# Gate matrix of a PEER layer stored as groups of 16 expert rows with the tokens outside, instead of expert rows with the tokens inside

## The chip, the cores and the metric

The kernel runs on one core of one Trainium2 chip. The metric is device time in microseconds (us) of one execution. The kernel before took 1841.26 us, the median of three runs (1835.47 to 1842.40).

## The reference, cut to what matters

One decoder layer for 576 tokens (512 of a prompt, 64 of samples), model width 1024. After attention, convolution and their output projection comes PEER: each token picks, in each of 8 heads, 16 of 16384 single-neuron experts. Expert e = i * 128 + j has a row u[e] and a row v[e].

```python
best_s, pos = lax.top_k(cand_s, PEER_TOPK)
idx = jnp.take_along_axis(cand_i, pos, axis=-1)
gate = jax.nn.softmax(best_s, axis=-1)
...
hu = jnp.einsum('chkd,cd->chk', jnp.take(u, ib, axis=0), xb)
act = jax.nn.gelu(hu, approximate=False) * gb
return jnp.einsum('chk,chkd->cd', act, jnp.take(v, ib, axis=0))
```

## The kernel before, in words

The tokens are split. For the last 192 tokens (tiles 3 and 4) the rows of u and v are gathered from memory one pick at a time: 384 rows of 128 tokens x 1024, each an indirect DMA issued by POOL into an eight-slot ring and one VectorE instruction (L1349 for u, L1353 for v). For the first 384 tokens PEER is computed densely, over all experts, in 128 blocks n of 128 experts:

- the U part: `dense_u(n)` multiplies a block of u with the tokens (24 matmuls of 384 columns, L711), ScalarE applies gelu into `gest` (`step`, L942), and SyncE stores it to `gelu_matrix` in memory (`store_gelu`, L402);
- the gate matrix: for each token an expert-by-expert matrix of gates, 128 partitions (i) x 128 rows (j);
- the V part: the gelu block and the gate block of n are loaded and multiplied on VectorE into `mt` (L1420), and 18 matmuls of 512 columns (L783) add the product with a block of v into PSUM.

Weights and activations of both dense parts are split in a high and a low half: ScalarE rounds (`high`, L916; `ah`, L1026), VectorE subtracts (`low`, L1234; `al`, L1428). `raw`, the block as it comes from memory, has three buffers; `hi`, `lo`, `mt`, `ah` and `al` have two.

The gate matrix is built in 64 batches of six tokens (`NBAT`, `BATCH`). For each batch VectorE writes two sets of one-hot rows, `gA` and `gB` (L1397, three buffers, `ABUF`), ScalarE scales `gA` by the gates (L997, six instructions), TensorE multiplies the two for each token (L761), giving 128 x 128 per token in PSUM, and ScalarE copies the six results into `Gs` (L1013). Four batches fill one block of 24 tokens (`TBLK`), of which there are 16 (`NBLK`), and SyncE then stores it to `gate_matrix` (L469). Between the batches each engine's program has a share of other work written out by hand: 54 blocks of the U part (`u_at`), 126 gathered rows of u and 26 of v (`batch_rows`). Below, "the gate stage" is the stretch of these 64 batches, about 893 to 1252 us of the profiled execution, and "the V stage" what follows the last five blocks of the U part, about 1283 to 1837 us.

In the V stage the gates are used in groups g of 16 expert rows j (`JG`): `Gl` holds two groups, each with 16 blocks of 24 tokens. Step n uses row n % 16 of group n // 16. The sixteen block loads of group g + 1 are issued one a step during group g, each right behind the multiplication of that step (`sp.wait_ge(s_mu, n + 1)`, then `load_gelu(n + EG)`, then `load_gates(n // JG + 1, n % JG)`), so the last one of a group is issued after the multiplication of its 16th step and is needed by the next one. VectorE's program for a step is: `mt` (L1420), one gathered row of v, `low`, `al`, and in about three steps of ten (`v_rows`) one more gathered row; 166 rows in 128 steps. ScalarE's is `high` for step n, which waits until TensorE is through with step n - 2, and then `ah`. TensorE waits for `low` and `al` of the step.

Of the kernel before, what the change touches and what calls it, by code (L numbers as in the profile page):

```python
# [5 lines left out]
ALU = mybir.AluOpType  # L6
# [8 lines left out]
P = 128  # L15
# [18 lines left out]
NKEY = 128  # L34
# [11 lines left out]
TBLK = 24  # L46
NBLK = DT // TBLK
BATCH = 6
ABUF = 3
NBAT = DT // BATCH  # L50
JG = 16
NG = NKEY // JG
# [117 lines left out]
def hymba_peer(nc, xT_d, wblk_d, cols_d, maskp_d, masks_d, ident_d, ckT_d, cv_d, state_d, keysT_d, u_d, v_d, uT_d,  # L170
# [7 lines left out]
    with ExitStack() as ctx:  # L178
        def sb(name, shape, dt=F32):
            return ctx.enter_context(nc.sbuf_tensor(name, shape, dt))[:]  # L180
# [4 lines left out]
        ps = [ctx.enter_context(nc.psum_tensor(f"ps{i}", [P, 1024], F32)) for i in range(4)]  # L185
# [11 lines left out]
        with ExitStack() as gates:  # L197
            def gb(name, shape, dt=F32):
                return gates.enter_context(nc.sbuf_tensor(name, shape, dt))[:]

            kT3 = gb("kT3", [P, 3, DT])
            A = gb("gA", [P, ABUF, BATCH, NKEY])
            B = gb("gB", [P, ABUF, BATCH, NKEY])
            Gs = gb("Gs", [P, 2, NKEY, TBLK])

        Gl = sb("Gl", [P, 2, NBLK, JG, TBLK])
        cols = sb("cols_sb", [P, NCOL])
        ident = sb("ident_sb", [P, P])
        epst = sb("epst", [P, 1])
# [157 lines left out]
        def _(sp):  # L367
# [47 lines left out]
                sp.dma_start(gel[:, n % EG, :], ge_d[k][:, (n % 2) * DT:(n % 2 + 1) * DT]).then_inc(e_in[n % EG], 16)  # L415

            def load_gates(g, b):
                sp.dma_start(Gl[:, g % 2, b].rearrange("p j t -> p (j t)"),
                             gm_d[b, :, g * JG:(g + 1) * JG, :].rearrange("p j t -> p (j t)")).then_inc(s_gl[g % 2], 16)

            for c in range(DC):
                sp.dma_start(hT[:, c, :], xT_d[:, c, :]).then_inc(x_in[c], 16)
# [40 lines left out]
            for b in range(NBAT):  # L463
                for n in range(u_at(b), u_at(b + 1)):
                    after_u(n)
                if b % (TBLK // BATCH) == TBLK // BATCH - 1:
                    i = b // (TBLK // BATCH)
                    sp.wait_ge(s_gev, b + 1)
                    sp.dma_start(gm_d[i].rearrange("p j t -> p (j t)"),  # L469
                                 Gs[:, i % 2].rearrange("p j t -> p (j t)")).then_inc(s_gst, 16)  # L470

            for n in range(U_TAIL, NKEY):
                after_u(n)
# [30 lines left out]
        def _(pe):  # L504
# [49 lines left out]
            n = nblk[0]  # L554
# [199 lines left out]
            for b in range(NBAT):  # L754
                pe.wait_ge(s_ab, 2 * b + 2)
                pe.wait_ge(s_ag, b + 1)
                if b >= ABUF:
                    pe.wait_ge(s_gev, b - ABUF + 1)
                for t in range(BATCH):
                    c = (t // 3) * 512 + (t % 3) * NKEY  # L760
                    mm = nc.tensor.matmul(ps[b % ABUF][:, c:c + NKEY], A[:, b % ABUF, t, :], B[:, b % ABUF, t, :],  # L761
                                          start=True, stop=True)
                mm.then_inc(s_gmm, 1)
                for n in range(u_at(b), u_at(b + 1)):
                    dense_u(n)
# [23 lines left out]
        def _(act):  # L789
# [212 lines left out]
            for b in range(NBAT):  # L1002
                i = b // (TBLK // BATCH)
                o = b % (TBLK // BATCH) * BATCH
                if b + 1 < NBAT:
                    apply_gates(b + 1)
                act.wait_ge(s_gmm, b + 1)
                if o == 0 and i >= 2:
                    act.wait_ge(s_gst, 16 * (i - 1))
                dst = Gs[:, i % 2, :, o:o + BATCH].rearrange("p j (a t) -> p a t j", a=2)  # L1010
                src = ps[b % ABUF][:, :].rearrange("p (a c) -> p a c", a=2)[:, :, 0:3 * NKEY].rearrange(
                    "p a (t j) -> p a t j", t=3)
                nc.scalar.activation(dst, src, ACT.Copy).then_inc(s_gev, 1)  # L1013
                if b in GELU_AFTER:
                    gelu_rows(GELU_AFTER[b])
                for n in range(u_at(b), u_at(b + 1)):
                    step(n)
# [43 lines left out]
        def _(dve):  # L1061
# [351 lines left out]
            for n in range(NKEY):  # L1413

                g = n // JG
                dve.wait_ge(e_in[n % EG], 16 * (n // EG + 1))
                dve.wait_ge(s_gl[g % 2], 16 * NBLK * (g // 2 + 1))
                if n >= 2:
                    dve.wait_ge(s_al, n - 1)
                nc.vector.tensor_tensor(mt[:, n % 2, :].rearrange("p (a b) -> p a b", a=NBLK),  # L1420
                                        gel[:, n % EG, :].rearrange("p (a b) -> p a b", a=NBLK),
                                        Gl[:, g % 2, :, n % JG, :], ALU.mult).then_inc(s_mu, 1)
                rows = list(range(v_rows(n), v_rows(n + 1)))
                for r in rows[:1]:
                    row(r)
                low(NKEY + n)
                dve.wait_ge(s_ah, n + 1)
                nc.vector.tensor_tensor(al[:, n % 2, :], mt[:, n % 2, :], ah[:, n % 2, :].bitcast(F32),  # L1428
                                        ALU.subtract).then_inc(s_al, 1)
                for r in rows[1:]:  # L1430
                    row(r)
                if UROW + NPICK in range(v_rows(n), v_rows(n + 1)):
                    dve.wait_ge(g_used, UROW + NPICK)
                    dve.sem_inc(s_y, 1)
# [98 lines left out]
```

## Time and profile before

| | |
|---|---|
| median of three runs | 1841.26 us (1835.47 to 1842.40) |
| profiled execution | 1849.16 us, span in the trace 1847.3 us |
| granted TensorE clock, mean | 0.953 |
| busy: PE, DVE, ACT, POOL | 1669.8, 1432.0, 770.1, 550.0 us |
| DMA over the span | 477.45 MB, mean 258 GB/s |

PE is TensorE (PEld its weight loads), DVE VectorE, ACT ScalarE, POOL GpSimd, SP SyncE, which here only issues DMAs. All times are of one profiled execution; the busy share of an engine over the whole span is an average over stages with different limits, so the stages are read apart. "Idle before" is time in which the engine did nothing before an instruction, and the name behind the arrow what ended it, as far as the semaphores show.

### The profile page before, as it was taken

What the parts mean: (1) busy time and instruction counts of PE and PEld (TensorE: products, weight loads), DVE (VectorE), ACT (ScalarE), POOL (GpSimd) and SP (SyncE); (2) the same over time, 40 slices, a digit from 0 to 9 for tenths busy, and PEclk for the clock granted to TensorE, in tenths of its full rate; (3) what the DMA queues carried; (4) which work ended last, traced back from release to release, by engine and by line L of the source; (5) the groups of instructions that cost most, each with busy time, mean ns of one, the idle gap of its engine ahead of it and who ended that gap; (6) DMA issues with size and microseconds to landing.
All of it is one profiled execution on the core that took longest, in us unless ns stands there. A gap on an engine that the chain in (4) does not pass through costs nothing.

```text
span 1847.3 us, 23140 instructions
## 1 busy us (share of the span) xinstructions
PE 1669.8 (90%) x8361; PEld 1447.9 (78%) x8361; DVE 1432.0 (78%) x2657; ACT 770.1 (42%) x1274; POOL 550.0 (30%) x395
## 2 busy tenths in 40 slices
PE   7887678989699998999889898998999999999997
PEld 5766446769697877999889898998877877877876
DVE  3466854338778999787899999994888888988976
ACT  3222112212242222444789888883333333333332
POOL 0000000000011333111477676661344443443430
PEclk9998887999899999999999999999999999999999
DMA  6110500125275877777699999999999999999985
GB/s 192 46 46 1 66 1 13 50 68 194 89 247 184 277 281 228 248 235 234 216 415 407 406 413 402 381 403 389 363 371 371 375 362 381 387 358 365 379 306 184
DMA packets 164360, 477.45 MB, mean 258 GB/s; under 512 B 28063, under 2 KB 61535, under 8 KB 162071
## 3 DMA queue, kind: packets, MB, share of 16 engines
q1 hardware_dynamic: 108951, 274.63, 42.7%
q0 software_dynamic: 55296, 201.35, 28.7%
q8 instruction: 67, 1.10, 0.2%
q14 instruction: 46, 0.38, 0.1%
HBM read 420.93 MB, written 54.42 MB: 257 GB/s over the span
## 4 chain that ended last, share of the span: by engine, by line
PE 55%; DVE 33%; issue 5%; ACT 3%; DMA 2%; SPq 0%; DVEq 0%; ACTq 0%
PE ps L783 24%; PE ps L711 14%; PE ps L524 9%; DVE ring L1349 8%; DVE lo L1234 4%; DVE acc L1353 2%; DVE gA L1397 2%; DVE gB L1397 2%; DVE cacc L1457 2%; DVE tsi L1246 2%; PE ps L536 2%; DVE tsi L1249 2%; DVE sm L1247 2%; DVE tsv L1248 1%; DMA gelu_matrix<-gest 1%
## 5 line engine op out<-in xcount | busy, mean ns | idle before, releaser
L1057 POOL DMA_INDIRECT ring<-in_u,idx x192 | 281.6, 1467 | 889.1 <-DVE ijg L1329 528.4
L1234 DVE TENSOR_TENSOR lo<-raw,hi 128x1024 fp32r<-128x1024 f32 x256 | 312.9, 1222 | 138.3 <-ACT hi L916 132.2
L916 ACT ACTIVATE hi<-raw 128x1024 fp32r<-128x1024 f32 x256 | 270.4, 1056 | 330.7 <-PE ps L783 323.9
L711 PE MATMUL ps<-xh,hi 128*128 128x384 f32 x1024 | 356.1, 348 | 28.2 <-DVE lo L1234 20.2
L1057 POOL DMA_INDIRECT ring<-in_v,idx x192 | 266.9, 1390 | 369.4 <-DVE acc L1353 351.2
L711 PE MATMUL ps<-xl,hi 128*128 128x384 f32 x1024 | 348.0, 340 | 0.0
L711 PE MATMUL ps<-xh,lo 128*128 128x384 f32 x1024 | 347.5, 339 | 0.0
L783 PE MATMUL ps<-hi,ah 128*128 128x512 f32 x768 | 241.6, 396 | 23.1 <-DVE al L1428 23.0
L1353 DVE SCALAR_TENSOR_TENSOR acc<-ring,hu,acc 128x1024 f32<-128x1024 f32 x192 | 245.6, 1279 | 1.6
L783 PE MATMUL ps<-lo,ah 128*128 128x512 f32 x768 | 240.0, 394 | 0.0
L783 PE MATMUL ps<-hi,al 128*128 128x512 f32 x768 | 239.6, 394 | 0.0
L1349 DVE CUSTOM_DVE_ANT_0 ring<-ring,xtok 128x1024 f32<-128x1024 f32 x192 | 226.2, 1216 | 0.3 <-DVE hu L1349 0.3
L711 PEld LDWEIGHTS ps<-xh,hi 128*128 128x128 f32 x1024 | 197.7, 193 | 31.0 <-DVE lo L1234 22.9
L711 PEld LDWEIGHTS ps<-xl,hi 128*128 128x128 f32 x1024 | 197.2, 193 | 0.0
L711 PEld LDWEIGHTS ps<-xh,lo 128*128 128x128 f32 x1024 | 196.6, 192 | 0.0
L783 PEld LDWEIGHTS ps<-hi,ah 128*128 128x128 f32 x768 | 146.2, 191 | 56.6 <-DVE lo L1234 20.9
L783 PEld LDWEIGHTS ps<-lo,ah 128*128 128x128 f32 x768 | 146.6, 191 | 31.1
L783 PEld LDWEIGHTS ps<-hi,al 128*128 128x128 f32 x768 | 146.3, 190 | 31.0
L942 ACT ACTIVATE gest<-ps 128x384 f32<-128x384 f32 x128 | 63.4, 495 | 251.8 <-PE ps L711 210.7
L681 PE MATMUL ps<-xn,wring 128*128 128x192 f32 (+1 forms) x512 | 133.6, 416 | 5.6 <-DVE xn L1224 5.6
L1013 ACT ACTIVATE Gs<-ps 128x768 f32<-128x768 f32 x64 | 132.3, 2067 | 0.5 <-PE ps L761 0.5
L761 PE MATMUL ps<-gB,gA 128*128 128x128 f32 x768 | 103.3, 288 | 32.0 <-issue 18.4
(176 smaller groups left out, 1971.8 us busy)
## 6 DMA issues: line engine op xcount, KB each, us to landing
raw<-in_uT SPq DMA_DIRECT2D x128, 512.0 KB
raw<-in_v SPq DMA_DIRECT2D x128, 512.0 KB
wring<-in_wblk SPq DMA_DIRECT2D x48, 512.0 KB
gelu_matrix<-gest SPq DMA_DIRECT2D x64, 384.0 KB
gate_matrix<-Gs SPq DMA_DIRECT2D x16, 1536.0 KB
Gl<-gate_matrix SPq DMA_DIRECT2D x128, 192.0 KB
gel<-gelu_matrix SPq DMA_DIRECT2D x128, 192.0 KB
wring<-in_wblk SPq DMA_DIRECT2D x16, 256.0 KB
```

The costliest lines, as they stand in the source:

```text
L524: mm = nc.tensor.matmul(out[:, a * 512:a * 512 + HALF], w, rhs[:, k, a * HALF:(a + 1) * HALF], start=(k == 0), stop=(k == kc - 1))
L681: mm = nc.tensor.matmul(out[:, 0:w], wring[:, n % RING, k * P:(k + 1) * P], xn[:, k, t0:t0 + w], start=(k == 0), stop=(k == DC - 1))
L711: mm = nc.tensor.matmul(out, a[:, n % 2, w], b[:, c, :], start=(c == 0 and k == 0), stop=(c == DC - 1 and k == 2))
L761: mm = nc.tensor.matmul(ps[b % ABUF][:, c:c + NKEY], A[:, b % ABUF, t, :], B[:, b % ABUF, t, :], start=True, stop=True)
L783: mm = nc.tensor.matmul(ps[t][:, h * 512:(h + 1) * 512], a[:, n % 2, w], b[:, n % 2, h * 512:(h + 1) * 512], start=False, stop=(n == NKEY ...
L916: nc.scalar.activation(hi[:, s % 2, :], raw[:, s % RAWS, :], ACT.Copy).then_inc(s_hi, 1)
L1013: nc.scalar.activation(dst, src, ACT.Copy).then_inc(s_gev, 1)
L1057: pool.indirect_dma_start(ring[:, r % SLOTS, :], None, table, bass.IndirectOffsetOnAxis(idx[:, t, c:c + 1], 0)).then_inc(g_in[r % SLOTS], 16)
L1234: nc.vector.tensor_tensor(lo[:, s % 2, :], raw[:, s % RAWS, :], hi[:, s % 2, :].bitcast(F32), ALU.subtract).then_inc(s_lo, 1)
L1349: nc.vector.tensor_tensor_reduce(got, got, xtok[:, t, :], 1.0, 0.0, ALU.mult, ALU.add, hu[:, t, c:c + 1]).then_inc(g_used, 1)
L1353: nc.vector.scalar_tensor_tensor(out=acc[:, t, :], in0=got, scalar=hu[:, t, c:c + 1], in1=acc[:, t, :], op0=ALU.mult, op1=ALU.add).then_in ...
L1397: nc.vector.tensor_tensor(dst[:, b % ABUF], iota.unsqueeze(1).broadcast_to([P, BATCH, NKEY]), kT3[:, half, tok:tok + BATCH].unsqueeze(2).b ...
```

## The change

The layout of the gate matrix is changed in all four places where it is touched: in `Gs`, in memory, in `Gl`, and in the operand of the multiplication.

- In `Gs` a token's 128 gates of a partition lay 24 elements (96 bytes) apart, with the tokens next to each other. Now they lie in eight groups of 16 adjacent elements (64 bytes); within a group the tokens follow one another, so the groups of a block are 1536 bytes each.
- The store writes the same 12288 contiguous bytes of each partition, and a load still reads and writes 1536 contiguous bytes of each partition. The number and size of the DMAs and their places in the queue are unchanged.
- In PSUM the six results of a batch lay as three and three, each three at the start of a bank of 512; now they lie one behind the other, four in the first bank and two in the second.
- The multiplication L1420 read 16 runs of 24 adjacent gates for its 384 tokens. Now it reads 384 single gates, each 16 elements (64 bytes) from the one before. Its other input and its output are as before.

No instruction is added, removed or moved on any engine: the programs of PE, DVE, ACT, POOL and SP have the same instructions in the same order with the same waits, and only the access patterns named above differ.

```diff
-            Gs = gb("Gs", [P, 2, NKEY, TBLK])
+            Gs = gb("Gs", [P, 2, NG, TBLK, JG])
-        Gl = sb("Gl", [P, 2, NBLK, JG, TBLK])
+        Gl = sb("Gl", [P, 2, NBLK, TBLK, JG])
...
             def load_gates(g, b):
-                sp.dma_start(Gl[:, g % 2, b].rearrange("p j t -> p (j t)"),
-                             gm_d[b, :, g * JG:(g + 1) * JG, :].rearrange("p j t -> p (j t)")).then_inc(s_gl[g % 2], 16)
+                sp.dma_start(Gl[:, g % 2, b].rearrange("p t j -> p (t j)"),
+                             gm_d[b].rearrange("p j t -> p (j t)")[:, g * JG * TBLK:(g + 1) * JG * TBLK]).then_inc(
+                                 s_gl[g % 2], 16)
...
                     sp.dma_start(gm_d[i].rearrange("p j t -> p (j t)"),
-                                 Gs[:, i % 2].rearrange("p j t -> p (j t)")).then_inc(s_gst, 16)
+                                 Gs[:, i % 2].rearrange("p g t j -> p (g t j)")).then_inc(s_gst, 16)
...
                 for t in range(BATCH):
-                    c = (t // 3) * 512 + (t % 3) * NKEY
+                    c = t * NKEY
...
-                dst = Gs[:, i % 2, :, o:o + BATCH].rearrange("p j (a t) -> p a t j", a=2)
-                src = ps[b % ABUF][:, :].rearrange("p (a c) -> p a c", a=2)[:, :, 0:3 * NKEY].rearrange(
-                    "p a (t j) -> p a t j", t=3)
+                dst = Gs[:, i % 2, :, o:o + BATCH, :].rearrange("p g t j -> p t g j")
+                src = ps[b % ABUF][:, 0:BATCH * NKEY].rearrange("p (t g j) -> p t g j", t=BATCH, g=NG)
                 nc.scalar.activation(dst, src, ACT.Copy).then_inc(s_gev, 1)
...
                 nc.vector.tensor_tensor(mt[:, n % 2, :].rearrange("p (a b) -> p a b", a=NBLK),
                                         gel[:, n % EG, :].rearrange("p (a b) -> p a b", a=NBLK),
-                                        Gl[:, g % 2, :, n % JG, :], ALU.mult).then_inc(s_mu, 1)
+                                        Gl[:, g % 2, :, :, n % JG], ALU.mult).then_inc(s_mu, 1)
```

## Rows read from the trace of the kernel before

**Rows 1.** Stretches: length, busy us (instructions) of each engine, granted clock, DMA share, GB/s

```profile
900.00:1000.00 100.00, 93.20 (x595) 92.69 (x595) 100.00 (x141) 88.30 (x158) 73.13 (x44) 0.96 0.97 382
...
1280.00:1840.00 560.00, 534.75 (x2304) 439.15 (x2304) 473.50 (x553) 191.79 (x261) 213.65 (x157) 0.98 0.94 352
```

**Rows 2.** Groups of instructions, shapes kept apart: count | busy us, mean ns | idle before

```profile
L1013 ACT ACTIVATE Gs<-ps 128x768 f32<-128x768 f32 x64 | 132.3, 2067 | 0.5 <-PE ps L761 0.5
L942 ACT ACTIVATE gest<-ps 128x384 f32<-128x384 f32 x128 | 63.4, 495 | 251.8 <-PE ps L711 210.7 <-DMA gelu_matrix<-gest 22.0 <-issue 19.1
L849 ACT ACTIVATE PTb<-ps 128x1024 f32<-128x1024 f32 x6 | 6.1, 1024 | 49.7 <-PE ps L601 49.7
...
L761 PE MATMUL ps<-gB,gA 128*128 128x128 f32 x768 | 103.3, 288 | 32.0 <-issue 18.4 <-DVE gA L1397 9.4 <-ACT gA L997 4.2
```

**Rows 3.** Waits between 893 and 1252 us: us in total, times, longest

```profile
DVE lo L1234 <- ACT hi L916: 6.0, 4, 2.1
...
ACT gest L942 <- DMA gelu_matrix<-gest: 12.8, 6, 5.5
```

**Rows 4.** Timeline before one of these waits, SP, ACT and DVE: start, length, idle before

```profile
1004.95 0.33 SPq L469 DMA_DIRECT2D gate_matrix<-Gs  x1
...
1005.79 1.33 SPq L402 DMA_DIRECT2D gelu_matrix<-gest  x1
...
1019.48 0.49 ACT L942 ACTIVATE gest<-ps 128x384 f32<-128x384 f32 x1 [5.49 <-DMA gelu_matrix<-gest]
...
1020.94 1.23 DVE L1234 TENSOR_TENSOR lo<-raw,hi 128x1024 fp32r<-128x1024 f32 x1 [2.11 <-ACT hi L916]
```

**Rows 5.** Timeline from the last batch to the V stage, ACT and SP

```profile
1249.14 2.08 ACT L1013 ACTIVATE Gs<-ps 128x768 f32<-128x768 f32 x1
...
1251.25 0.33 SPq L469 DMA_DIRECT2D gate_matrix<-Gs  x1
...
1270.63 0.42 SPq L402 DMA_DIRECT2D gelu_matrix<-gest  x1
...
1279.74 0.49 ACT L942 ACTIVATE gest<-ps 128x384 f32<-128x384 f32 x1 [7.80 <-DMA gelu_matrix<-gest]
```

**Rows 6.** Groups of VectorE's instructions, shapes kept apart, columns as in rows 2

```profile
L1420 DVE TENSOR_TENSOR mt<-gel,Gl 128x384 f32<-128x384 f32 x128 | 70.6, 552 | 29.3 <-issue 26.6 <-DMA gel<-gelu_matrix 2.7
L1234 DVE TENSOR_TENSOR lo<-raw,hi 128x1024 fp32r<-128x1024 f32 x256 | 312.9, 1222 | 138.3 <-ACT hi L916 132.2 <-issue 2.9
```

**Rows 7.** Timeline of VectorE over steps 15 to 18 of a group

```profile
1479.76 0.55 DVE L1420 TENSOR_TENSOR mt<-gel,Gl 128x384 f32<-128x384 f32 x1
...
1489.14 0.56 DVE L1420 TENSOR_TENSOR mt<-gel,Gl 128x384 f32<-128x384 f32 x1 [4.02 <-issue]
...
1492.42 0.55 DVE L1420 TENSOR_TENSOR mt<-gel,Gl 128x384 f32<-128x384 f32 x1
1492.89 1.28 DVE L1353 SCALAR_TENSOR_TENSOR acc<-ring,hu,acc 128x1024 f32<-128x1024 f32 x1
1494.08 1.22 DVE L1234 TENSOR_TENSOR lo<-raw,hi 128x1024 fp32r<-128x1024 f32 x1
...
1495.69 0.55 DVE L1420 TENSOR_TENSOR mt<-gel,Gl 128x384 f32<-128x384 f32 x1
```

**Rows 8.** Timeline of ScalarE in steady steps of the V stage

```profile
1501.11 1.06 ACT L916 ACTIVATE hi<-raw 128x1024 fp32r<-128x1024 f32 x1 [2.61 <-PE ps L783]
...
1529.67 1.07 ACT L916 ACTIVATE hi<-raw 128x1024 fp32r<-128x1024 f32 x1 [2.61 <-PE ps L783]
```

**Rows 9.** Chain of waits: TensorE's restarts after the first and the seventh group

```profile
1353.52 4.34 PE ps L783 x18
...
1768.51 68.17 PE ps L783 x288
```

**Rows 10.** Waits between 1300 and 1837 us, VectorE: us in total, times, longest

```profile
DVE lo L1234 <- ACT hi L916: 46.6, 74, 3.3
DVE mt L1420 <- issue: 26.6, 7, 4.4
```

## The prediction

> **What bounds the kernel now.** I read the stretches first [rows 1]. In the gate stage VectorE is the full engine, 100.00 us of the 100 between 900 and 1000 us, ScalarE follows at 88.30, and TensorE, though busy by its records for 93.20, waits for the other two between batches. In the V stage TensorE is busy for 534.75 of 560 us, VectorE for 473.50, ScalarE for only 191.79. The change touches ScalarE in the first stage and VectorE in the second, so both are worked out apart.
>
> In the steady part of the V stage ScalarE starts `hi` eight times in 28.56 us, always released by TensorE, so a step takes 28.56 / 7 = 4.08 us [rows 8]. VectorE's own program for such a step is shorter: from one `mt` to the next without a wait 1495.69 - 1492.42 = 3.27 us with one gathered row, whose place in it is 1.19 us [rows 7]. With 166 rows in 128 steps there are 0.297 more rows a step, so 3.27 + 0.297 x 1.2 = 3.63 us. VectorE has 0.45 us a step to spare, and it shows as 46.6 us of waits of `lo` for `hi` [rows 10]. TensorE bounds the steady steps.
>
> Once a group there is another limit. The last load of the next group's gates is issued behind the 16th `mt`, and the next `mt` starts 1489.14 - 1479.76 = 9.38 us after it, with VectorE idle for the last 4.02 us [rows 7], 26.6 us in seven boundaries [rows 10]. TensorE's restarts after the first and the seventh boundary give the length of a group: (1768.51 - 1353.52) / 6 = 69.2 us [rows 9]. Were VectorE never to wait for `hi`, a group would take 15 x 3.63 + 9.38 = 63.8 us.
>
> **The copy L1013.** It takes 2067 ns for 768 elements, while contiguous activations out of PSUM take 495 ns for 384 and 1024 ns for 1024 [rows 2]. The slope is 529 / 640 = 0.83 ns an element with about 178 ns fixed, so the copy pays (2067 - 178) / 768 = 2.46 ns an element where 0.83 would be the price of adjacent ones. What is peculiar in it is the 96-byte step of its output. In the new layout its output comes in runs of 16 adjacent elements, and I price it at 178 + 768 x 0.83 = about 815 ns: 1.25 us less each, 64 x 1.25 = 80 us less of ScalarE's work. The bounds are 0 and 1.25 us saved; I take 1.25: the row of 1024 elements, which crosses the end of a PSUM bank, shows no price for that, and that jumps between runs of 16 cost nothing is my choice.
>
> Almost none of the 80 us lies on the path. VectorE is full there, with work that the change leaves alone. All it can gain is its waits for `hi`, 6.0 us in four pieces [rows 3]. One of them shows how they come about: SyncE stands at the store of a gate block until the fourth copy is done, behind it stand a load of `raw` and a store of gelu, the latter issued at 1005.79; ScalarE waits for it until 1019.48, and VectorE at 1020.94 [rows 4]. A copy that ends 1.25 us earlier moves the queue up by that. Still, 13.7 us from issue to release is mostly a loaded memory path, with the DMA share at 0.97 in the stretch before [rows 1], and that load stays. Behind the stage the last copy (1249.14), the last gate store (1251.25), the gate loads behind it, the gelu store (1270.63) and the gelu step (1279.74) are one chain into the V stage, which moves up by 1.25 us with the copy [rows 5]. So the gate stage gives between 0 and 6.0 + 1.25 = 7.3 us; I take 4. TensorE's write of six results to other columns of PSUM and the DMAs, the same in number and bytes, I cost at nothing: nothing about them changes that could be slower, and TensorE has its waits for VectorE as cover in that stage; without that cover L761 slower by a tenth would cost a tenth of its 103.3 us [rows 2].
>
> **The multiplication L1420.** It takes 552 ns for 384 elements, and `lo` takes 1222 ns for 1024 [rows 6], so VectorE runs at 670 / 640 = 1.05 ns an element. Its second input is now read at a 64-byte step. No instruction of VectorE in the trace reads singly at such a step. The bounds are no cost at all (the rate it has in all its other forms) and the increment of the copy, (2.46 - 0.83) x 384 = 0.63 us. Since the row nearest to it, and the only one of single fp32 elements far apart, shows 2.46 ns an element, I take that rate as one of the memory, whatever the engine: (2.46 - 1.05) x 384 = 0.54 us more, `mt` at about 1.09 us. Call this extra x.
>
> What x does to a group: VectorE's own length becomes 63.8 + 16x, and the length set by TensorE 69.2 + 2x, because around a boundary the 16th `mt` (before the last load) and the next one (after it) are both on the path. They cross at x = 0.38. Below that only 2x a boundary is paid, above it VectorE sets the group. With x = 0.54 it is 63.8 + 8.6 = 72.4 us, 3.2 more than 69.2. Seven groups end in a boundary: 22.4 us. The eighth has none: 15 steps x (3.63 + 0.54 - 4.08) = 1.4 us. Sum of the V stage: +24 us. ScalarE's `ah` waits for `mt` but is needed only by `al`, behind a row and `low`, so its chain costs nothing more; the row gathers of POOL and the loads behind `s_mu` on SP come later by x each step, with four buffers of `gel` and eight of the ring as cover.
>
> **Weighing the skill.** By the trace a step of 96 bytes costs 2.46 ns an element on ScalarE's output [rows 2]. The Trainium skill, "Vector Engine (DVE) Microarchitecture Reference", section 5.2, gives for VectorE 2.50 to 2.51 ns a column where both sources, or the output alone, step by 24 words, but only 1.73 where one source hops by 4 KiB each element and the rest is contiguous. With 1.73 the extra would be an estimated (1.73 - 1.05) x 384 = 0.26 us, under the crossing; with 2.50 an estimated 0.56. The trace of before shows neither for VectorE, and the step of 64 bytes stands in neither line.
>
> **Sum.** 24 - 4 = +20 us: 1849.16 + 20 = 1869 for the profiled execution. That execution was 7.9 us above the median of the runs shown, so the forecast against the median is 1841.26 + 20 = 1861.
>
> **Rivals.**
> 1. *VectorE reads at a middling price, x up to 0.38, and its slack covers it.* For it: 0.45 us of idle time a step [rows 7, 8]. Against it: the rate of the copy. With x = 0.27, half of what I take, it costs 7 x 0.54 = 3.8 us, and some 2 more where two-row steps follow closely, less 4 from the gate stage: 1843, a range of 1836 to 1849.
> 2. *The read costs nothing and the kernel gets faster.* The place is ScalarE's copy and the chain of waits behind it, the price of the V stage is zero, and it decides as long as 14x stays under the gate stage's gain, so for x below about 0.3 if that gain is 4. For it: the copy is slow on its output, and nothing in the trace shows a slow input; an output that must put single words into a wider line may be a case of its own. Against it: the small share of ScalarE on the path. Time: 1841 - 4 = 1837, at best 1834 with all 7.3 us. The Trainium skill, "VectorE: DVE Perf Modes", in its part on the one-element mode, says that this mode makes no assumptions and that fp32 and weird strides work in it. By that rule, this rival is the outcome; no row of the trace contradicts it.
> 3. *The step of 64 bytes costs more than the one of 96.* With x = 0.63 a group is 73.9 us and the V stage 7 x 4.7 + 15 x 0.18 = +36; with nothing gained in the gate stage the time is 1877. If the price were a whole copy-like fixed wait per element more (x = 0.8), a group would be 76.6 and the time about 1895. Against it: no row is that slow.
> 4. *The copy doesn't get faster,* since its output still has two levels of jumps. Then the gate stage gives 0, and with x = 0.54 the time is 1865. The new output's runs speak against it.
>
> **Chances.** Forecast, with rival 4 as a variant of it: 0.56 (0.06 of it rival 4). Rival 1: 0.20. Rival 2: 0.12. Rival 3: 0.12. The range 1837 to 1877 leaves out the better half of rival 2, some of rival 1 and the upper half of rival 3, together near 0.2. The likeliest case has its own range, 1851 to 1872: its V stage lies between +15 (x = 0.47) and +31 (x = 0.6), its gate stage between 0 and -5. Half a per cent, 9.2 us, is about what a measurement of this kernel can tell from no change. Faster than 1832 needs rival 2 with more than the chain seen can give: 0.05. Slower than 1850.5: the forecast but for its low end, rival 3, a rest of rival 1: 0.54 + 0.12 + 0.02 = 0.68. Between them 0.27.
>
> **What would show it.** In the profile after: L1013 at about 0.82 us and ScalarE at about 690 us in all; L1420 at 1.09 us instead of 552 ns; the waits of `lo` for `hi` in the V stage down from 46.6 us to a few; TensorE waiting inside the groups for `al` or `lo`, and its restarts 72.4 us apart; the 26.6 us at the boundaries unchanged; in the gate stage VectorE waiting less than 6.0 us for `hi`. An `mt` under 0.9 us proves the forecast wrong, and so does a group of 70 us with an `mt` over a microsecond, since then VectorE's slack was not what I count.

## The result, and the profile after

The changed kernel takes 1853.62 us, the median of 11 runs (1842.35 to 1858.31), against 1842.46 us of the kernel before in the same call (11 runs). The ratio on record is 1.0044, 95% interval 1.0023 to 1.0065: 8 us slower (4 to 12), where the two medians alone lie 11 us apart; the text goes by the ratios. Forecast were 20 us and a time of 1861 us. The profiled execution took 1849.48 us, 4 us under the median of its kind, and the profiled one of before 7 us over its own, so the two traces, 0.3 us apart, don't show the loss in their totals. They show what happened to each step.

The stretches after, columns as in [rows 1]:

```profile
900.00:1000.00 100.00, 94.35 (x600) 93.83 (x600) 100.00 (x141) 65.56 (x155) 73.10 (x44) 0.96 0.97 382
1280.00:1840.00 560.00, 532.42 (x2301) 435.73 (x2299) 501.16 (x549) 188.39 (x255) 299.46 (x157) 0.98 0.94 348
```

ScalarE fell from 88.30 to 65.56 us in the stretch of the gate stage with VectorE still at 100.00, and VectorE rose from 473.50 to 501.16 us in the V stage. POOL rose there from 213.65 to 299.46 us, which I had not expected. The groups, columns as in [rows 2, 6]:

```profile
L1013 ACT ACTIVATE Gs<-ps 128x768 f32<-128x768 f32 x64 | 50.9, 796 | 2.4 <-PE ps L762 2.4
L1420 DVE TENSOR_TENSOR mt<-gel,Gl 128x384 f32<-128x384 f32 x128 | 105.5, 824 | 31.8 <-issue 28.7 <-DMA gel<-gelu_matrix 3.1
L1057 POOL DMA_INDIRECT ring<-in_v,idx x192 | 354.3, 1845 | 286.8 <-DVE acc L1353 272.8 <-issue 9.8 <-DVE hu L1349 4.2
```

The copy takes 796 ns instead of 2067, against 815 forecast. The multiplication takes 824 ns instead of 552, so x is 0.27 us, half of the 0.54 that I took. The waits between 893 and 1252 us:

```profile
DVE lo L1234 <- ACT hi L917: 2.6, 1, 2.6
```

They were 6.0 us in four pieces [rows 3]. All four are gone: the one left is the wait that stood just behind the end of this stretch before. The trace of before, then that of after:

```profile
1254.12 1.22 DVE L1234 TENSOR_TENSOR lo<-raw,hi 128x1024 fp32r<-128x1024 f32 x1 [2.65 <-ACT hi L916]
```

```profile
1248.15 1.22 DVE L1234 TENSOR_TENSOR lo<-raw,hi 128x1024 fp32r<-128x1024 f32 x1 [2.63 <-ACT hi L917]
```

The V stage's first `mt` starts at 1270.30 us in this trace, at 1275.95 before: 5.7 us earlier, where I took 4. All `mt` of the V stage, before and then after (count, shortest/mean/longest in ns, first and last start in us):

```profile
L1420 DVE TENSOR_TENSOR mt<-gel,Gl x128: 548/551/559, 1275.9 to 1827.2; 128x384 f32<-128x384 f32 x128
```

```profile
L1420 DVE TENSOR_TENSOR mt<-gel,Gl x128: 801/824/854, 1270.3 to 1827.7; 128x384 f32<-128x384 f32 x128
```

From the first to the last it is 551.3 us before and 557.4 after. So the gain of the gate stage is there, and a V stage 6.1 us longer takes it back. VectorE's steps in the V stage after, as in [rows 7]:

```profile
1475.05 0.82 DVE L1420 TENSOR_TENSOR mt<-gel,Gl 128x384 f32<-128x384 f32 x1
...
1484.39 0.80 DVE L1420 TENSOR_TENSOR mt<-gel,Gl 128x384 f32<-128x384 f32 x1 [3.98 <-issue]
...
1487.91 0.81 DVE L1420 TENSOR_TENSOR mt<-gel,Gl 128x384 f32<-128x384 f32 x1
...
1491.44 0.83 DVE L1420 TENSOR_TENSOR mt<-gel,Gl 128x384 f32<-128x384 f32 x1
```

A step with one gathered row is 1491.44 - 1487.91 = 3.53 us, 0.26 more than before, and still under TensorE's 4.08.

### The profile page after: what moved, and what is told of

Read it like the earlier page. It is cut to its first block, busy times and chain, and to the rows that moved or that the text cites. A ratio compares the mean times of both kernels' runs of the same rounds, so it can differ in the third digit from the quotient of the medians.

```text
span 1847.7 us, 23140 instructions
## 1 busy us (share of the span) xinstructions
PE 1669.4 (90%) x8361; PEld 1445.4 (78%) x8361; DVE 1463.5 (79%) x2657; ACT 692.6 (37%) x1274; POOL 638.9 (35%) x395
## 4 chain that ended last, share of the span: by engine, by line
PE 51%; DVE 36%; issue 5%; DMA 4%; ACT 3%; SPq 0%; DVEq 0%; POOL 0%; ACTq 0%
PE ps L784 21%; PE ps L712 13%; DVE ring L1349 9%; PE ps L525 9%; DVE lo L1234 4%; DVE acc L1353 2%; DVE gA L1397 2%; DVE gB L1397 2%; DVE cacc L1457 2%; PE ps L537 2%; DVE tsi L1246 2%; DVE tsi L1249 2%; DVE sm L1247 2%; DVE tsv L1248 1%; DMA gelu_matrix<-gest 1%
## 5 line engine op out<-in xcount | busy, mean ns | idle before, releaser
L1057 POOL DMA_INDIRECT ring<-in_v,idx x192 | 354.3, 1845 | 286.8 <-DVE acc L1353 272.8
L1420 DVE TENSOR_TENSOR mt<-gel,Gl 128x384 f32<-128x384 f32 x128 | 105.5, 824 | 31.8 <-issue 28.7
```

The source lines that it names most:

```text
L1057: pool.indirect_dma_start(ring[:, r % SLOTS, :], None, table, bass.IndirectOffsetOnAxis(idx[:, t, c:c + 1], 0)).then_inc(g_in[r % SLOTS], 16)
```

## The experiments

All ratios are to the kernel before in the same call, with 95% intervals; 0.001 is 1.8 us.

**The two halves of the change apart.** `mul_only` is the kernel before with another view in the multiplication, `copy_only` the changed one (views shortened):

```diff
-  Gl[:, g % 2, :, n % JG, :]                                   # before
+  Gl[:, g % 2] as "p (b t j) -> p b t j" [:, :, :, n % JG]     # mul_only
-  Gl[:, g % 2, :, :, n % JG]                                   # after
+  Gl[:, g % 2] as "p (b j t) -> p b j t" [:, :, n % JG, :]     # copy_only
```

> The kernel before, but the multiplication L1420 reads its gates singly at a 64-byte step, so it multiplies by gates of other tokens and experts; the copy and the layout stay as before. Theory A (the changed kernel is slower only through the multiplication, whose extra 0.27 us is mostly covered by VectorE's slack): mt at 0.82 us, the V stage longer by 14 x 0.27 = 3.8 us at the boundaries and by what close two-row steps cost, together +4 to +14 us, nothing gained in the gate stage, so +4 to +14 us against before, more than the changed kernel itself by the gate stage's 4 to 6 us. Rival B (the multiplication is covered, and what makes the changed kernel slower is a shift of the transfers against each other that begins in the gate stage): within 3 us of before.

Measured: 1.0039 (1.0017 to 1.0061), +7 us, with the multiplication at 825 ns. Theory A's range holds it; rival B's (3 us) ends just where the interval begins.

> The changed kernel, but the multiplication L1420 reads runs of 24 adjacent gates from the new layout, so it multiplies by gates of other tokens and experts; copy, store and loads are as changed. Theory A: the gate stage ends 4 to 6 us earlier as in the changed kernel, L1420 back at 0.55 us, V stage as before: -4 to -6 us against before. Rival B (the earlier gate stage is given back in the V stage by transfers): 0 to +8 us against before with a V stage longer than before's although L1420 takes 0.55 us.

Measured: 0.9975 (0.9952 to 0.9998), -4.6 us (-9 to 0), as theory A had it.

**Another way to a fast copy.** The kernel before with `dst = Gs[:, i % 2, :, o:o + BATCH]`, `src = ps[...][:, 0:768].rearrange("p (t j) -> p j t", t=BATCH)` and `c = t * NKEY`:

> The kernel before with its layout of the gate matrix and its multiplication; the copy L1013 goes through its elements in another order, experts outside and the six tokens inside: it writes runs of six adjacent elements (24 bytes) and reads PSUM at a step of 512 bytes, the six results lying one behind the other. If only the output's single elements make the copy slow, it takes about 0.8 us and the kernel has the gain of the gate stage without the slower multiplication: -4 to -6 us. If steps in PSUM cost as steps in the output do, the copy takes 1.5 to 2.1 us and the time is that of before within 3 us.

Measured: 0.9972 (0.9944 to 1.0000), -5 us; the copy takes 830 ns. The time alone would not exclude the other theory, the duration does: steps of 512 bytes in PSUM cost it next to nothing (830 against 796 ns); its single elements in the output did.

**What a step costs.** One profile, eight forms of each instruction, every form on a line of its own:

> The changed kernel with eight forms of the multiplication L1420, one for each n % 8 (adjacent gates; single gates 8, 16, 32, 64, 96 and 128 bytes apart; pairs of adjacent gates 128 bytes apart), and eight forms of the copy L1013, one for each block % 8 (adjacent; single elements 16, 32, 64, 96 and 128 bytes apart; pairs 192 bytes apart; runs of six from PSUM at 512 bytes); the gates used are others than the reference's. For the theory of my prediction that one rate of the memory holds for all engines, the multiplication at 96 bytes should take about 1.1 us although it takes 0.82 at 64. If VectorE's input simply costs less than ScalarE's output, 64, 96 and 128 bytes all take about 0.82 us. Adjacent forms and pairs: 0.55 us and 0.8 us.

The groups of that profile, multiplication first. L1462 is adjacent, L1464 to L1474 are 8, 16, 32, 64, 96 and 128 bytes apart, L1476 pairs 128 bytes apart. L1022 is adjacent, L1024 to L1036 are 16, 32, 64, 96 and 128 bytes apart, L1038 pairs 192 bytes apart. The multiplications at 96 and 128 bytes read 192 elements twice, the others 384 different ones.

```profile
L1472 DVE TENSOR_TENSOR mt<-gel,Gl 128x384 f32<-128x384 f32 x16 | 17.7, 1109 | 0.0
L1033 ACT ACTIVATE Gs<-ps 128x768 f32<-128x768 f32 x8 | 16.5, 2064 | 0.0
L1468 DVE TENSOR_TENSOR mt<-gel,Gl 128x384 f32<-128x384 f32 x16 | 14.3, 892 | 0.0
L1474 DVE TENSOR_TENSOR mt<-gel,Gl 128x384 f32<-128x384 f32 x16 | 14.2, 885 | 0.0
L1466 DVE TENSOR_TENSOR mt<-gel,Gl 128x384 f32<-128x384 f32 x16 | 13.5, 844 | 0.0
L1027 ACT ACTIVATE Gs<-ps 128x768 f32<-128x768 f32 x8 | 13.4, 1674 | 0.0
L1470 DVE TENSOR_TENSOR mt<-gel,Gl 128x384 f32<-128x384 f32 x16 | 13.2, 824 | 0.0
L1036 ACT ACTIVATE Gs<-ps 128x768 f32<-128x768 f32 x8 | 12.7, 1589 | 0.0
L1024 ACT ACTIVATE Gs<-ps 128x768 f32<-128x768 f32 x8 | 12.5, 1560 | 0.0
L1030 ACT ACTIVATE Gs<-ps 128x768 f32<-128x768 f32 x8 | 12.3, 1543 | 0.0
L1462 DVE TENSOR_TENSOR mt<-gel,Gl 128x384 f32<-128x384 f32 x16 | 8.9, 555 | 35.8 <-issue 32.0 <-DMA gel<-gelu_matrix 3.8
L1476 DVE TENSOR_TENSOR mt<-gel,Gl 128x384 f32<-128x384 f32 x16 | 8.9, 554 | 0.0
L1464 DVE TENSOR_TENSOR mt<-gel,Gl 128x384 f32<-128x384 f32 x16 | 8.8, 552 | 0.0
...
L1038 ACT ACTIVATE Gs<-ps 128x768 f32<-128x768 f32 x8 | 6.9, 863 | 0.0
...
L1022 ACT ACTIVATE Gs<-ps 128x768 f32<-128x768 f32 x8 | 6.4, 800 | 0.8 <-PE ps L762 0.8
```

Both theories of the expectation were half right. The 96-byte step does have one rate on both engines: 1.05 + (1109 - 552) / 384 = 2.50 ns an element on VectorE, (2064 - 178) / 768 = 2.46 on ScalarE, and my figure of 1.09 us would have been right for it. But 96 bytes is a special step. At 16, 32, 64 and 128 bytes the two take 1.76 to 1.94 and 1.78 to 1.95 ns. Single elements 8 bytes apart and pairs 128 bytes apart cost VectorE nothing, and pairs 192 bytes apart cost ScalarE 63 ns of 800. The figures of the Trainium skill that the prediction names ("Vector Engine (DVE) Microarchitecture Reference", section 5.2) agree with this: its 2.50 to 2.51 for a step of 24 words is stated for both sources or the output, and one source alone shows 2.50 here; its 1.73 for one source hopping by 4 KiB is close to the 1.76 of the 64-byte step.

**The same with x = 0.56.** The multiplication reads `Gl[...][0:4608]` at every 24th element, 192 elements twice:

> The kernel before, with the multiplication L1420 reading single gates 96 bytes apart (the wrong gates, 192 of them twice); by the sweep it takes 1.11 us, so x = 0.56 us. My sum (VectorE's own length of a group 63.8 + 16x against TensorE's 69.2 + 2x) gives groups of 72.8 us and 7 x 3.6 + 15 x 0.11 = +27 us against before. If what VectorE's extra costs is simply proportional to it (7 us for 0.27 us), +15 us. If transfers set the V stage rather than either engine, +7 to +10 us as with x = 0.27.

Measured: 1.0063 (1.0040 to 1.0086), +12 us, multiplication 1106 ns. My sum (+27) is out; the transfers' +7 to +10 and the proportional +15 both lie in the interval.

**Both halves, old layout.** Fast copy as above, slow multiplication as in `mul_only`:

> The kernel before with the copy's experts outside and tokens inside (0.83 us) and with the multiplication reading singly at a 64-byte step (0.82 us, the wrong gates): both of the change's effects without its layout. If the two add up, +7.2 - 5.2 = +2 us against before. If there is something in having both (the earlier start of the V stage is lost where VectorE has less slack), or the changed kernel's +8 us is the true sum, +6 to +10 us. If it comes out at +2 while the changed kernel is at +8, the layout itself costs something.

Measured: 1.0050 (1.0031 to 1.0069), +9 us, like the changed kernel. So no cost of the layout in memory shows, within some 5 us. The halves alone sum to +2.6 us, with some 6 us of uncertainty on that sum, so that they don't add up is suggested by this and not shown.

> Copy with experts outside (0.83 us) and multiplication reading single gates 96 bytes apart (1.11 us, wrong gates). If gate stage and V stage add up: +11.6 with the slow copy, less 5.2 = +6 us. If the gain of the fast copy is lost whenever VectorE has little slack (as +9 instead of +2 at 0.82 us suggests), +12 to +18 us.

The edit is that of the 96-byte multiplication in the kernel with the fast copy. Measured: 1.0055 (1.0031 to 1.0079), +10 us, with the slow copy it was +12. The gain of 5 us that the fast copy has with the fast multiplication is not seen in the time with the slow one; but +6 is just within the interval too, so this is open.

**Groups of 2 expert rows.** `Gs [P, 2, NKEY // 2, TBLK, 2]`, `Gl [P, 2, NBLK, JG // 2, TBLK, 2]`:

> The changed kernel with groups of 2 expert rows instead of 16 in Gs, memory and Gl (tokens outside a pair, a load still 1536 adjacent bytes): the copy writes pairs of adjacent elements, the multiplication reads single gates 8 bytes apart. By the sweep the copy takes 0.86 us and the multiplication 0.55 us. If only the two durations matter, it is where the copy alone was, 0.9975 of before (-5 us), though tokens lie outside as in the changed kernel. If the layout in memory has a price of its own, +3 us or more against before.

Measured: 0.9984 (0.9959 to 1.0009), multiplication 552 ns, copy 869 ns. That is -3 us (-8 to +2): the interval holds the first expectation (-5) and not the second (+3 or more), so tokens outside cost nothing that shows.

**The boundary off the path.** SyncE's loads of the next group's gates come closer together:

```diff
-   if n // JG + 1 < NG:
-       load_gates(n // JG + 1, n % JG)
+   if n // JG + 1 < NG and n % JG < NBLK // 2:       # early
+       load_gates(n // JG + 1, 2 * (n % JG))
+       load_gates(n // JG + 1, 2 * (n % JG) + 1)
+   # spread: n % JG < 12; blocks 2k and 2k + 1 for k < 4, then block k + 4
```

> The changed kernel, but SyncE issues two gate loads of the next group in each of the first eight steps of a group instead of one in each of the sixteen, so the last has eight steps to land. If the boundary wait is the last load alone, the 28.7 us of waits of mt at the boundaries go and with them 20 to 28 us of the kernel (-12 to -20 us against before), and the 2x at each boundary is off the path. If the memory path is the limit there, the loads that come closer together delay raw and gel by as much and the time stays within 5 us of the changed kernel (0 to +12 against before).

> The kernel with the copy's experts outside and tokens inside (fast copy, multiplication at 0.55 us), and gate loads two a step as in the other run of this call. If VectorE's slack covers the extra 0.27 us of the multiplication once the boundaries are off the path, this is within 4 us of the changed kernel with early gate loads, less the clash of two-row steps, -15 to -30 us against before. If the extra is uncovered within the groups, this is 7 to 12 us faster than the changed kernel with early gate loads.

Measured: 0.9945 (0.9922 to 0.9968) and 0.9912 (0.9885 to 0.9938), -10 and -16 us. The waits of `mt` at the boundaries are gone, but less than their 28 us was won, and the second kernel is only 6 us (within some 6) ahead of the first, between the two expectations. ScalarE waits for `raw` for 97 and 102 us in the V stage, against 15 in the changed kernel.

> Fast copy with experts outside, multiplication at 0.55 us, and the sixteen gate loads of the next group issued in the first twelve steps (two in each of the first four, then one). With two in each of the first eight steps, ScalarE waited 102 us for raw and the boundary was free. If the crowding of the loads costs, this is 3 to 8 us faster than that, 0.987 to 0.989 of before; if the memory path is full over the whole group, it is the same, 0.991.

> The changed kernel (multiplication 0.82 us) with the gate loads of the next group spread over the first twelve steps. Against the same spread with the multiplication at 0.55 us (0.9834 of before). If VectorE's slack of 0.45 us a step covers the extra 0.27 us once the boundary is off the path: 0.983 to 0.985. If the extra costs within the groups, by clashes of close two-row steps or through the transfers: 7 to 13 us more, 0.987 to 0.990.

Measured: 0.9834 (0.9804 to 0.9864), -31 us, and 0.9876 (0.9846 to 0.9907), -23 us. The first won more than either expectation; it computes what the reference does and has the lowest time of this study. With the slow multiplication the time is 8 us longer, but the two come from two calls and their intervals overlap, so 8 is uncertain by 8. The waits of ScalarE in the V stage, first the fast, then the slow one:

```profile
ACT hi L918 <- DMA raw<-in_v: 35.4, 12, 4.4
```

```profile
ACT hi L919 <- DMA raw<-in_v: 79.4, 27, 4.1
```

> Fast copy, multiplication reading single gates 96 bytes apart (1.11 us, wrong gates), gate loads spread over the first twelve steps. VectorE's step is then 3.63 + 0.56 = 4.19 us against TensorE's 4.08: by my sum without boundaries 128 x 0.11 = +14 us against the spread kernel with the fast multiplication (0.991 of before). If the crossing is not there and the cost is proportional to the extra, it is twice what the changed kernel with spread loads costs over the fast one.

Measured: 1.0089 (1.0059 to 1.0120), 47 us more than the fast multiplication in the other call, where I expected 14 for VectorE's step over TensorE's. Its V stage takes 568.2 us from the first `mt` to the last, as long as without the spread loads (568.3), though the boundaries no longer wait. The trace points to another limit in their place. POOL's gather instruction, of which one ran 2.62 us behind VectorE's two-input instructions before, takes 2.90 us after and here:

```profile
1359.42 3.18 POOL L1058 DMA_INDIRECT ring<-in_v,idx  x1 [0.64 <-DVE acc L1354]
1363.25 3.18 POOL L1058 DMA_INDIRECT ring<-in_v,idx  x1 [0.65 <-DVE acc L1354]
```

That is 2.62 + x each time. POOL is busy for 499.0 us with the 192 gathers of v, its share of the chain of waits in the V stage is about 23%, the largest there, and for the first time VectorE waits for gathered rows:

```profile
DVE acc L1354 <- DMA ring<-in_v,idx: 19.1, 5, 7.1
```

No run relieved POOL with this multiplication, so this is read from one trace and not tested.

**Four buffers of raw.** Both spread kernels with `RAWS = 4`, `SLOTS = 7`, so that what `low` releases late has a step more to land:

> The changed kernel with spread gate loads, and with four buffers of raw and seven slots in the ring instead of three and eight (the memory is full otherwise). Theory: the extra 0.27 us of the multiplication is not covered because low and so the next load of raw come later, with raw's three buffers too few for a load of 7 us and more on a full memory path (79 us of waits of hi for raw against 35). With four buffers those waits go for both multiplications, and this and the kernel of the same call with the fast multiplication are within 3 us of one another. Rival: the extra acts through POOL, whose gather instruction grows from 2.62 to 2.90 us because it waits for VectorE's two-input instructions, or through VectorE's own clashes; then this is still 6 to 9 us slower than its partner.

> The partner: fast copy with experts outside, multiplication at 0.55 us, spread gate loads, four buffers of raw and seven slots in the ring. Where raw's landing bounds the steps, it is some 3 to 8 us faster than with three buffers (0.979 to 0.982 of before). If it is TensorE alone that bounds, 0.983 as with three buffers. If seven slots are too few for the gathered rows, slower than 0.983, with waits of VectorE for ring.

Measured: 0.9881 (0.9858 to 0.9904) and 0.9875 (0.9853 to 0.9898), medians 1818.58 and 1818.28 us. The difference of 8 us has gone, with the multiplication at 826 and 551 ns. Neither trace has a wait for `raw`, and the V stage of the slow one looks like this:

```profile
1280.00:1800.00 520.00, 519.97 (x2287) 430.44 (x2288) 499.99 (x547) 186.32 (x253) 316.89 (x158) 1.00 0.99 376
```

TensorE is busy throughout, at full granted clock, with VectorE at 499.99 of 520 us. The V stages of the four spread kernels, with three buffers the fast and the slow multiplication, with four the fast and the slow:

```profile
L1421 DVE TENSOR_TENSOR mt<-gel,Gl x128: 545/551/558, 1265.6 to 1791.0; 128x384 f32<-128x384 f32 x128
```

```profile
L1422 DVE TENSOR_TENSOR mt<-gel,Gl x128: 801/828/849, 1271.2 to 1801.9; 128x384 f32<-128x384 f32 x128
```

```profile
L1421 DVE TENSOR_TENSOR mt<-gel,Gl x128: 547/551/558, 1271.4 to 1794.2; 128x384 f32<-128x384 f32 x128
```

```profile
L1422 DVE TENSOR_TENSOR mt<-gel,Gl x128: 793/826/861, 1272.4 to 1794.7; 128x384 f32<-128x384 f32 x128
```

They are 525.4 and 530.7 us long with three buffers, 522.8 and 522.3 with four. So within the V stage the slow multiplication costs 5 us with three buffers and nothing with four, though POOL's gathers are as long as before: with the loads spread, its cost goes through the load of `raw`, as far as one profile for each kernel can show it, and neither through VectorE nor through POOL. The whole times bear this out only in part. They are equal with four buffers, but against its own three-buffer kernel the slow one did not gain (0.9881 against 0.9876) and the fast one lost (0.9875 against 0.9834), each pair in two calls with some 4 thousandths of uncertainty. The profile of the fast three-buffer kernel was ahead before its V stage began (1265.6 against 1271.4 us), where the multiplication plays no part. Why is open; the seven slots of the ring changed together with `raw`, and no run changed one alone.

## Why the prediction was wrong

**The copy and the gate stage: right.** 796 ns against 815; -4.6 and -5 us alone against -4; VectorE's waits fell as named. In the profiles of the thirteen kernels with a fast copy (the sweep left out) the V stage's first `mt` starts at 1270.2 us in the mean (1265.6 to 1272.4), in the three with the slow copy at 1274.2 (1273.3 to 1275.9): 4 us, with either multiplication.

**The step that failed: "I take that rate as one of the memory, whatever the engine".** One rate for both engines was right at 96 bytes, but I carried a row of a 96-byte step over to one of 64 bytes. With 1.76 ns instead of 2.46 x is 0.27 us, under the crossing, and rival 1 is what happened: x = 0.27 was its own number. An `mt` under 0.9 us was also my own sign that the forecast is wrong, and it is 0.82. That the time of 1853.62 us came within 8 us of 1861, and within the range of 1837 to 1877 that holds rival 1 as well, says nothing for the mechanism. Rival 2 (no cost) is out by the same row: what it leaned on says only that such steps work, not that they are free.

**The second error: rival 1's price.** It had +2 us in all, measured are +8, and +7 for the multiplication alone, where I had 7 x 0.54 plus 2 = 6, less 4. So the halves alone match my terms within a few microseconds, and the sum of both does not; whether that is more than the uncertainty of some 6 us stays open. The longer V stage itself can be traced, to stalls at the boundaries and to the granted clock behind them, of which my sum knew nothing. The 8.2 us from TensorE's restart on, at each of the seven boundaries, in the kernel with the fast copy and fast multiplication (two steps are 36 matmuls):

```profile
1349.17:1357.37 8.20, 8.10 (x34) 6.38 (x35) 8.20 (x11) 2.00 (x3) 5.76 (x4) 1.00 0.93 328
1417.40:1425.60 8.20, 8.20 (x36) 6.79 (x37) 8.20 (x11) 2.00 (x3) 5.29 (x4) 1.00 0.91 327
...
1622.80:1631.00 8.20, 8.20 (x29) 6.64 (x30) 7.10 (x8) 2.00 (x3) 4.75 (x4) 0.79 0.97 347
```

and with the same copy and the slow multiplication in the old layout:

```profile
1350.38:1358.58 8.20, 8.20 (x25) 6.51 (x26) 6.68 (x8) 1.77 (x3) 5.33 (x4) 0.67 0.89 324
1421.74:1429.94 8.20, 8.20 (x24) 6.54 (x25) 6.52 (x8) 1.63 (x3) 4.57 (x4) 0.65 0.91 295
1493.89:1502.09 8.20, 8.20 (x25) 6.55 (x26) 5.54 (x7) 1.84 (x3) 4.03 (x3) 0.67 0.92 326
```

The clock is at its level of 2.4 GHz for the whole stretch where the column says 1.00, and for a part of it at 1.2 GHz elsewhere. For each kernel: TensorE's mean idle time before the seven restarts; the restarts with 1.00 in the column; the matmuls that the seven stretches of 8.2 us lack of 7 x 36 = 252; the sum of both losses, the idle time seven times and each lacking matmul as 0.227 us (a step's 4.08 us over its 18 matmuls); and the V stage from its first `mt` to its last. A few matmuls are lacking at 1.00 too (33 or 34 of 36 in some stretches), so a difference of two or three means nothing.

| kernel | copy, mt (us) | mean idle (us) | restarts at full clock | lacking | both losses (us) | V stage (us) |
|---|---|---|---|---|---|---|
| before | 2.07, 0.55 | 2.6 | 3 of 7 | 34 | 26 | 551 |
| after | 0.80, 0.82 | 3.3 | 3 of 7 | 33 | 31 | 557 |
| mul_only | 2.07, 0.82 | 2.9 | 1 of 7 | 62 | 35 | 559 |
| copy_only | 0.80, 0.55 | 3.2 | 5 of 7 | 17 | 26 | 551 |
| fast copy, experts outside | 0.83, 0.55 | 2.7 | 5 of 7 | 15 | 23 | 547 |
| groups of 2 | 0.87, 0.55 | 2.6 | 4 of 7 | 24 | 24 | 549 |
| both, old layout | 0.83, 0.82 | 3.8 | none | 72 | 43 | 568 |
| mt at 96 bytes | 2.07, 1.11 | 3.0 | 2 of 7 | 40 | 30 | 570 |
| fast copy, mt at 96 bytes | 0.83, 1.11 | 3.3 | none | 49 | 34 | 568 |

In the first seven rows the two losses account for the V stage: against before they differ by -3 to +17 us and the stage by -4 to +17, never more than 2 us apart. With the multiplication at 0.55 us the mean stall is 2.8 us, at 0.82 it is 3.3, which is my 2x a boundary, though single kernels overlap (3.2 with the fast, 2.9 with the slow one); the rest of the two losses is the clock. In the last two rows the losses leave some 9 to 15 us of the longer stage unexplained, and these lie inside the groups, where by the sum VectorE is the limit at x = 0.56.

The record also holds the mean granted clock of every execution, and this does not rest on one profile each. Over 100 executions of the kernel before, in five calls, it is 0.9560, and an execution with 0.001 less is 1.7 us longer (correlation -0.90). The means of the others, from 7 to 12 executions each and uncertain by 1 to 2 us in these terms: `mul_only` 0.9538, after 0.9529, both in the old layout 0.9517; and 0.9560 for both kernels with `mt` at 96 bytes. By the slope, with the stalls that go with it, the clock is worth about +4 us in `mul_only`, +5 in the changed kernel and +7 in both halves in the old layout, of the +7, +8 and +9 us measured, and nothing at 96 bytes. So the 64-byte multiplication costs in large part by a lower clock, and the 96-byte one otherwise. For the copy this can't be divided: `copy_only` and the fast copy with experts outside have 0.9578 and 0.9576, some 3 us, and start the V stage 4 us earlier, with -5 us measured for each within some 5. No run held the clock fixed, and why x = 0.27 lowers it and x = 0.56 does not is open, so the clock's part is a likely cause and not a shown one. With no stall at all and four buffers of `raw` the slow multiplication costs nothing, which fits it.

**The third error: 9.38 us for every boundary.** [rows 7] shows the longest but one of seven. The mean in the trace of before is 8.1 us (7.2 to 9.8), so VectorE's own length of a group is 62.6 + 16x and the crossing lies at x = 0.47. For x = 0.56 that gives 71.5, and the profile of the 96-byte kernel has 72.1 a group; its first group, bound by the start of the stage, does not grow. With +12 us measured instead of +27, the step's arithmetic was over by a factor of two even for its own x. With 8.1 us and six growing groups it gives 6 x (71.5 - 69.2) + 15 x 0.11 = +15, which the interval (7 to 16) holds.

**A slip.** Rival 3 at x = 0.8 is 7 x 7.4 + 15 x 0.35 = +57 us, so 1898 and not 1895.

**The chances.** I gave the likeliest case 0.56 and rival 1 0.20. The two rows of the sum that decide between them, 96 and 64 bytes, differ in a number that I had called a choice. The figure of 1.73 ns of the Trainium skill ("Vector Engine (DVE) Microarchitecture Reference", section 5.2) that the prediction named in a sentence beside the sum gives an estimated x of 0.26 and so the length of the multiplication; the time would still have come out at rival 1's +2 us instead of +8.

## What to carry to other kernels

A price per element is bound to its step: single fp32 elements 96 bytes apart cost 2.5 ns, at 64 or 128 bytes 1.8 to 1.9, while pairs and VectorE's 8-byte step cost little or nothing here (at most 63 ns of 800), so measure the step you are going to use, or keep pairs adjacent on both sides. An engine that stands beside the full one can be relieved of 80 us and the kernel gains 5. Before pricing slack in steady steps, look at what the other engine's instructions release: here one late gate load a group and, behind it, the three buffers of `raw` set what the slack was worth at 0.82 us, and moving that load was worth some 25 us (0.9834 against 0.9972, in two calls). Compare the mean granted clock of all executions before you put a small difference down to an engine.

## What the runs showed of the hardware that I had not expected

- Where POOL's indirect DMA instruction started inside a run of VectorE's two-input TENSOR_TENSOR instructions (`lo`, `al`, `mt`), it mostly ended only behind that run: 71 of 78 before and 97 of 109 after, between 1285 and 1800 us. Where it started outside one it took 0.94 us, in all 78 cases before. Behind a full run it took 2.62, 2.90 and 3.18 us with the multiplication at 0.55, 0.82 and 1.11 us. The mean over the gathers of v went from 1390 to 1845 ns.
- ScalarE read PSUM at a 512-byte step, writing runs of six, nearly as fast as adjacent elements (830 against 800 ns for 768).
- On both engines a 96-byte step is dearer than 16, 32, 64 and 128 bytes: 2.5 against 1.8 to 1.9 ns an element.
- Most of the spread of one kernel's executions goes with its mean granted clock: 1.7 us for 0.001, correlation -0.90 over 100 executions of the kernel before.
- Behind stalls of TensorE of 3.2 to 4.0 us the granted clock fell in all seven cases of one profile; in another it stayed at 1.00 behind 3.2 us. The length of the stall alone does not decide it.
